# The first norm and the projections of a time-mixing layer as one stage by blocks of 512 tokens, with the attention's bias lines made in the low-rank stage

## The reference

```
h   = x * rsqrt(mean(x*x, channels) + 1e-6) * norm_w
dx  = shift(h) - h                  # h of the token before, zero ahead of token 0
r, k, v = (h + dx*mu_i) @ w_in[i]   # 1024 x 1024 each
g   = silu((h + dx*mu_g) @ w_in[3])
decay, a = functions of low-rank products (rank 64) of h and dx
```

## Time and profile before

| what | value |
|---|---|
| three runs | 3332.02, 3344.9, 3361.51 us; median 3344.9 |
| the profiled execution's own time | 3351.66 us |
| its span, first to last instruction | 3349.6 us |
| mean granted TensorE clock | 0.931 of full speed |
| PE, DVE, ACT, POOL busy | 88%, 48%, 33%, 17% of the span |

### The profile page before, as it was taken

One profiled execution on the slowest core, in us unless ns is written; L12 is line 12 of the kernel. 1 busy time (PEld: TensorE's weight loads), 2 busy tenths in 40 slices (PEclk: granted clock), 3 DMA queues, 4 the chain that ended last, 5 costly groups with the idle time before them and its releaser, 6 DMA issues. The chain is left out here.

```text
span 3349.6 us, 79029 instructions
## 1 busy us (share of the span) xinstructions
PE 2946.6 (88%) x35086; PEld 2442.5 (73%) x35086; DVE 1591.4 (48%) x2641; ACT 1098.3 (33%) x2020; POOL 564.3 (17%) x379
## 2 busy tenths in 40 slices
PE   4599999998858888888876997999799997999699
PEld 1487888887547778778775775888677887777587
DVE  4423232342256666666763662222277402767672
ACT  2223332221644443544533441111032212545410
POOL 0222222210012322223220220000000000034231
PEclk8799999999969888898997998999899998999899
DMA  5213341211462323323213761101111215223672
GB/s 161 79 51 99 106 125 61 79 60 58 135 183 80 97 66 91 91 74 97 67 53 102 222 193 32 38 32 37 38 57 57 82 64 190 84 73 97 219 239 85
DMA packets 339816, 322.65 MB, mean 96 GB/s; under 512 B 13935, under 2 KB 257007, under 8 KB 337824
## 3 DMA queue, kind: packets, MB, share of 16 engines
q1 hardware_dynamic: 312528, 263.55, 25.6%
q10 hardware_dynamic: 23904, 46.16, 3.9%
q0 software_dynamic: 3056, 8.05, 1.0%
HBM read 199.77 MB, written 122.64 MB: 96 GB/s over the span
## 5 line engine op out<-in xcount | busy, mean ns | idle before, releaser
L343 PE MATMUL pj_ps<-pj_x_hi,pj_w_hi 128*128 128x512 f32 x1024 | 402.2, 393 | 69.9 <-DVE pj_x_lo L298 61.4
L343 PE MATMUL pj_ps<-pj_x_lo,pj_w_hi 128*128 128x512 f32 x1024 | 400.9, 392 | 0.0
L343 PE MATMUL pj_ps<-pj_x_hi,pj_w_lo 128*128 128x512 f32 x1024 | 400.8, 391 | 0.0
L343 PEld LDWEIGHTS pj_ps<-pj_x_hi,pj_w_hi 128*128 128x128 f32 x1024 | 193.8, 189 | 114.5 <-DVE pj_x_lo L298 62.6
L277 POOL TENSOR_TENSOR pj_x<-h 128x512 f32<-128x512 f32 x128 | 168.0, 1313 | 578.1 <-DVE pj_x_lo L298 515.6
L298 DVE TENSOR_TENSOR pj_x_lo<-pj_x,pj_x_hi 128x512 fp32r<-128x512 f32 x128 | 89.1, 696 | 356.6 <-ACT pj_x_hi L353 356.6
L343 PEld LDWEIGHTS pj_ps<-pj_x_lo,pj_w_hi 128*128 128x128 f32 x1024 | 193.9, 189 | 40.3
L343 PEld LDWEIGHTS pj_ps<-pj_x_hi,pj_w_lo 128*128 128x128 f32 x1024 | 193.6, 189 | 40.4
L2190 DVE CUSTOM_DVE_ANT_0 wa_sc<-wa_sps,wa_table 128x256 f32<-128x256 f32 (+2 forms) x384 | 124.0, 360 | 144.4 <-PE wa_sps L2121 144.3
L1666 PE MATMUL cv_ps<-h_hi,cv_w_hi 128*128 128x512 f32 x512 | 158.6, 391 | 20.8 <-DVE cv_w_lo L1709 20.8
L804 ACT CAST rw_x<-rw_ps 128x512 f16<-128x512 f32 x160 | 96.2, 601 | 201.8 <-PE rw_ps L1110 201.7
(11 more groups left out here) (260 smaller groups left out, 6468.0 us busy)
## 6 DMA issues: line engine op xcount, KB each, us to landing
proj<-pj_out ACTq DMA_DIRECT2D x128, 256.0 KB, 2.5
pj_w<-w_in SPq DMA_DIRECT2D x32, 512.0 KB, 4.1
proj<-lr_out SPq DMA_DIRECT2D x32, 512.0 KB, 4.5
no_w<-w_out SPq DMA_DIRECT2D x32, 512.0 KB, 5.2
partial<-wa_ob SPq DMA_DIRECT2D x48, 264.0 KB, 2.1
mo_part<-partial SPq DMA_DIRECT2D x16, 792.0 KB, 9.2
wa_vt<-v_rows SPq DMA_DIRECT2D x43, 260.0 KB, 3.4
h<-xT SPq DMA_DIRECT2D x8, 1024.0 KB, 13.0
```

The source lines that it names most:

```text
L343: mm = pe.matmul(ps[i][:], wp, xp, start=k == 0 and m == 0, stop=k == KT - 1 and m == len(parts) - 1)
```

## The change

norm_phase and rwkv_projections become `normed_projections`. h is loaded by blocks: SP loads blocks 0 and 1 as eight tiles of 128 x 512 each with the first tile of weights between them; POOL issues blocks 2 and 3 as one DMA each, block 2 once block 0 has landed and block 3 once block 1 has. The squares of blocks 0 and 1 are ACT's, summed by 16 calls on PE as before; those of blocks 2 and 3 POOL makes and adds up itself in steps 0 to 15 of q = 0, so that PE has one call each. The root is exp(-0.5 ln(.)) on ACT in PSUM; DVE scales from PSUM. Blocks 2 and 3 are scaled at steps 8 and 16. One output buffer serves the first 17 steps, as the other holds squares. The bias lines and the skew table move into rwkv_low_rank: PE makes the lines between down 0 and down 1, DVE copies them between its parts of h for blocks 0 and 1, POOL issues the DMAs. `basic` is loaded in the recurrence's start, and the block that zeroed column 0 is gone.

The diff, without the deleted norm_phase (shown above) and with the waits on `s_const` in the recurrence cut (48 becomes 64 in each engine):

```diff
-def rwkv_projections(nc, h, vec, w_in, proj):
+def normed_projections(nc, src, h, gain, vec, w_in, proj):
         w_hi = sb("w_hi", [128, KT, KT, 128], F32R)
...
         scaled = sb("scaled", [128, QT])
+        sq = [scaled, out_sb[1]]
+        ones, eps = sb("ones", [128, 128]), sb("eps", [128, 1])
         ps = [c.enter_context(nc.psum_tensor(f"pj_ps{i}", [128, QT], F32)) for i in range(2)]
+        var = [c.enter_context(nc.psum_tensor(f"pj_var{i}", [128, QT], F32)) for i in range(4)]
+        s_first = [[sem(f"h{b}{k}") for k in range(KT)] for b in range(2)]
+        s_last = [sem(f"h{b}") for b in range(2, 4)]
+        s_zero, s_ones, s_square, s_summed, s_part, s_total, s_log, s_rstd, s_normed = (sem(n) for n in (
+            "zero", "ones", "square", "summed", "part", "total", "log", "rstd", "normed"))
         s_diff, s_x, s_x_hi, s_x_lo, s_w_hi, s_w_lo = (sem(n) for n in ("diff", "x", "x_hi", "x_lo", "w_hi", "w_lo"))
...
+        def out_of(n):
+            return n % 2 if n > 2 * KT else 0
+        def tokens(b):
+            return slice(1 + QT * b, 1 + QT * (b + 1))
         def next_input(q, r, last):
...
             def difference(k, quarter, n):
                 t0 = quarter * QT
-                pool.wait_ge(s_x_lo, n)
+                if n < 4 * KT:
+                    pool.wait_ge(s_normed, n + 1)
+                pool.wait_ge(s_x_lo, n + 1)
                 pool.tensor_tensor(x[k % 2][:], h[:, k, t0:t0 + QT], h[:, k, t0 + 1:t0 + QT + 1],
...
             def body(q, r, last):
                 if at := next_input(q, r, last):
-                    difference(at[0], at[1], at[2] + 1)
+                    difference(at[0], at[1], at[2])
+                if q == 0 and r < 2 * KT:
+                    squares(2 + r // KT, r % KT)
+            def squares(b, k):
+                at = (2 * KT - 1) * (b - 2) + 2 * k
+                part = h[:, k, tokens(b)]
+                if k == 0:
+                    pool.wait_ge(s_last[b - 2], 16)
+                    if b == 2:
+                        pool.wait_ge(s_summed, 2 * KT)
+                    else:
+                        pool.wait_ge(s_total, 1)
+                    pool.tensor_tensor(sq[1][:], part, part, ALU.mult).then_inc(s_part, 1)
+                else:
+                    pool.wait_ge(s_part, at - 1)
+                    pool.tensor_tensor(sq[0][:], part, part, ALU.mult).then_inc(s_part, 1)
+                    pool.wait_ge(s_part, at)
+                    pool.tensor_tensor(sq[1][:], sq[1][:], sq[0][:], ALU.add).then_inc(s_part, 1)
+            pool.memset(ones[:], 1.0).then_inc(s_ones, 1)
+            pool.memset(eps[:], EPS).then_inc(s_ones, 1)
+            pool.memset(h[:, :, 0:1], 0.0).then_inc(s_zero, 1)
+            pool.wait_ge(s_zero, 1)
+            for b in range(2, 4):
+                pool.wait_ge(s_first[b - 2][KT - 1], 16)
+                pool.dma_start(h[:, :, tokens(b)], src[:, :, QT * b:QT * (b + 1)]).then_inc(s_last[b - 2], 16)
             pool.sem_inc(s_x_lo, 2)
             for k in range(KT):
-                difference(k, 0, k + 1)
+                difference(k, 0, k)
             blocks(pool, body)
         @block.vector
         def _(dve):
-            def mix(k, quarter, n, column):
-                i, t0 = quarter % 2, quarter * QT
+            def scale(b, k):
+                part = h[:, k, tokens(b)]
+                dve.wait_ge(s_rstd, b + 1)
+                dve.scalar_tensor_tensor(part, part, gain[:, k:k + 1], var[b][:],
+                                         ALU.mult, ALU.mult).then_inc(s_normed, 1)
+            def blend(k, quarter, n, column):
+                t0 = quarter * QT
                 dve.wait_ge(s_diff, n + 1)
...
                                          h[:, k, t0 + 1:t0 + QT + 1], ALU.mult, ALU.add).then_inc(s_x, 1)
+            def rest(k, quarter, n, column):
+                i = quarter % 2
                 dve.wait_ge(s_x_hi, n + 1)
...
             def body(q, r, last):
+                if q == 0 and r in (KT, 2 * KT):
+                    for k in range(KT):
+                        scale(1 + r // KT, k)
                 if at := next_input(q, r, last):
-                    mix(*at)
+                    blend(*at)
+                    rest(*at)
                 if at := next_weights(q, r, last):
...
+            def first(k):
+                return k, 0, k, V["mu_r"] + k
+            scale(0, 0)
+            scale(0, 1)
             weights(0, 0)
             for k in range(KT):
-                mix(k, 0, k, V["mu_r"] + k)
-            for j in range(1, FIRST):
+                blend(*first(k))
+                if k + 2 < KT:
+                    scale(0, k + 2)
+                rest(*first(k))
+            weights(0, 1)
+            weights(0, 2)
+            for k in range(KT):
+                scale(1, k)
+            for j in range(3, FIRST):
                 weights(0, j)
...
         def _(sp):
...
             sp.sem_inc(s_w_lo, 1)
-            with sp.Fori(0, 4) as q:
+            for b in range(2):
+                for k in range(KT):
+                    sp.dma_start(h[:, k, tokens(b)], src[:, k, QT * b:QT * (b + 1)]).then_inc(s_first[b][k], 16)
+                if b == 0:
+                    sp.dma_start(w[:], w_cols[:, :, 0:128]).then_inc(s_w, 16)
+            for j in range(1, KT):
+                sp.wait_ge(s_w_lo, j + 1)
+                sp.dma_start(w[:], w_cols[:, :, j * 128:j * 128 + 128]).then_inc(s_w, 16)
+            with sp.Fori(1, 4) as q:
                 for j in range(KT):
...
                 mm.then_inc(s_mm, 1)
+                if q == 0 and r in (KT - 1, 2 * KT - 1):
+                    b = 2 + r // KT
+                    pe.wait_ge(s_part, (2 * KT - 1) * (b - 1))
+                    pe.matmul(var[b][:], ones[:], sq[1][:], start=True, stop=True).then_inc(s_total, 1)
+            pe.wait_ge(s_ones, 2)
+            for b in range(2):
+                for k in range(KT):
+                    n = b * KT + k
+                    pe.wait_ge(s_square, n + 1)
+                    pe.matmul(var[b][:], ones[:], sq[n % 2][:], start=k == 0, stop=k == KT - 1).then_inc(s_summed, 1)
             blocks(pe, body)
         @block.scalar
...
+            def squares(b):
+                for k in range(KT):
+                    n = b * KT + k
+                    act.wait_ge(s_first[b][k], 16)
+                    if n >= 2:
+                        act.wait_ge(s_summed, n - 1)
+                    act.activation(sq[n % 2][:], h[:, k, tokens(b)], ACT.Square).then_inc(s_square, 1)
+            def inverse_root(b):
+                if b < 2:
+                    act.wait_ge(s_summed, KT * (b + 1))
+                else:
+                    act.wait_ge(s_total, b - 1)
+                act.activation(var[b][:], var[b][:], ACT.Ln, scale=1.0 / D, bias=eps[:]).then_inc(s_log, 1)
+                act.wait_ge(s_log, b + 1)
+                act.activation(var[b][:], var[b][:], ACT.Exp, scale=-0.5).then_inc(s_rstd, 1)
             def weights(q, j):
...
             def body(q, r, last):
+                if q == 0 and r in (KT, 2 * KT):
+                    inverse_root(1 + r // KT)
                 if at := next_input(q, r, last):
...
                 i, n = r % 2, q * PER + r
+                o = out_of(n)
                 act.wait_ge(s_mm, n + 2)
-                act.wait_ge(s_out[i], q * (8 * PER) + (16 * (r // 2) + 16))
+                act.wait_ge(s_out[o], 16 * sum(out_of(m) == o for m in range(n)) + 16)
+                if n == 2 * KT + 1:
+                    act.wait_ge(s_total, 2)
                 if last:
-                    act.activation(out_sb[i][:], ps[i][:], ACT.Sigmoid).then_inc(s_sig, 1)
+                    act.activation(out_sb[o][:], ps[i][:], ACT.Sigmoid).then_inc(s_sig, 1)
                 elif q == 1:
                     act.wait_ge(s_scaled, 16 * r)
-                    act.copy(out_sb[i][:], ps[i][:])
+                    act.copy(out_sb[o][:], ps[i][:])
                     act.activation(scaled[:], ps[i][:], ACT.Copy,
...
                 else:
-                    act.copy(out_sb[i][:], ps[i][:]).then_inc(s_ps_free, 1)
+                    act.copy(out_sb[o][:], ps[i][:]).then_inc(s_ps_free, 1)
                 act.wait_ge(s_ps_free, n + 3)
                 t0, j = r // KT * QT, r % KT
-                act.dma_start(proj_rows[q, :, j, t0:t0 + QT], out_sb[i][:]).then_inc(s_out[i], 16)
+                act.dma_start(proj_rows[q, :, j, t0:t0 + QT], out_sb[o][:]).then_inc(s_out[o], 16)
                 if q == 1:
...
             act.sem_inc(s_out[1], 16)
+            act.preload_act_table_set("natural_log_exp_and_others")
+            act.wait_ge(s_ones, 2)
+            squares(0)
+            inverse_root(0)
             weights(0, 0)
+            squares(1)
+            inverse_root(1)
             for k in range(KT):
...
             for i in range(2):
-                act.wait_ge(s_out[i], 8 * 4 * PER + 16)
```

(62 more changed lines are left out.)

84 lines of the change are left out of this document (removed).

## The result

| kernel | median of its runs | ratio to before, 95% interval |
|---|---|---|
| before, 4 runs | 3339.11 us (3332.02 to 3361.51) | 1 |
| changed, 4 runs | 3307.11 us (3291.77 to 3310.65) | 0.9879 [0.9836, 0.9922] |
| changed, once more, 5 runs | 3296.76 us | 0.9875 [0.9853, 0.9898] |

The ratio says 1.2% faster, some 40 us, with an interval clear of 1. The medians of the first set lie 32 us apart; in the second set the kernel before had 3341.44, so 45 us.

A forecast was written before the change was run, and what follows sets the result against it. PE bounds the kernel, so an earlier first product moves everything behind it: -62.5 + 1.9 + 2 + 3.3 + 3 + 0.5 = -51.8 us, 3299.9 for the profiled execution, median 3293, range 3275 to 3322.

The forecast's parts named there:

- The term for the table: Low-rank stage: skew table's DMAs meet the stores, part absorbed by ACT running four stores ahead; +3 us, bounds 0 and 16.
- T0: Start of the projections' first product: 113.1 us before, forecast 50.6 once it hangs on block 1, 62.5 us earlier.
- first steps: First 16 projection steps: two ones calls +1.9 us; ACT's first copy 0 to 3 us later, taken as +2.
- the 40 to 65: Whole kernel: the forecast's own band for the gain in us, given a chance of 0.71.
- Steps 8 and 16: Projections: root and eight scalings delay ACT's copy but cost PE nothing, with 1.9 us to spare.
- Lines: Low-rank stage: PE makes bias lines after down 0, then waits for DVE's copy and first part of block 1; +3.3 us.
- `basic`: Recurrence's start: loading it there costs one issue and a wait, +0.5 us (0 to 1).
- Its signs: Trace marks expected, among them a PE gap of about 3 us after down 0 and longer store waits in raised 0 only.
- 1: Rival: slow front (T0 57), steps losing 8 us and stores 16, all together; gain 21.8, time 3323; chance 0.17.
- the half-way case: Half of the way to the slow front and starved stores: time 3308 us.
- 2: Rival: block 1 lands late, crowded out by POOL's transfers; T0 68 or later, gain some 35 us, 3310; chance 0.05.
- 3: Rival: POOL bounds steps 0 to 15 through the port shared with DVE; slower, 3427 at steps of 13.8 us; chance 0.04.

The follow-up runs named there:

- `early_lines`: Changed kernel, but PE makes the bias lines before down 0 and ACT, not DVE, copies them out; ratio to before 0.9845, 3290.74 us.
- `pool_more`: Changed kernel with five more unread POOL multiplications of 128x192 in 14 of steps 0 to 15; ratio to before 0.9939, 3321.25 us.
- `weights_early`: `first_high` with weights 1 and 2 also split among the first mixes; ratio to before 0.9839, 3290.05 us.
- `first_high`: Changed kernel, but ACT alternates first high parts with block 1's squares and POOL issues block 3 after eight differences; ratio to before 0.9863, 3296.31 us.
- `best`: `weights_early` with `early_lines`, the skew table issued by SP ahead of its first store; ratio to before 0.9812, 3277.88 us.

## Why the prediction was right

The time was given as 3293, range 3275 to 3322, for a gain of 51.8; the first set of runs has its median at 3307, with a lowest run of 3292. Direction and range held, and so did the mechanism of the start. The term for the table did not, and luck hid part of that: T0 and the first steps came out 5.7 us better than forecast and paid for half of the 10.9 us that the table cost more. A gain of 32 by the medians or 40 by the ratio lies below or at the lower edge of the 40 to 65 that the forecast gave 0.71. Step by step:

- **T0**, forecast 50.6, measured 46.8. Block 0's sums took 7.19 to 17.5 (forecast 7.2 to 18.4), block 1's 16 records 9.1 us, 0.57 each in place of 0.70: the slow rate of the earlier trace rows belongs to the first records only. In block 0 the calls (two records each) began 1.7 to 1.8 us apart at first and 0.95 at the end; in block 1, where the granted clock was 0.50 at first (20 to 22), only the first two took 1.9 and 1.3. Block 1 had landed by 23.6 (forecast 25 to 28), so its loads bound nothing. The mixing took 16.1 us, and the 0.5 us for DVE's added scalings did not show. A gain of 66.3 instead of 62.5 in this pair; T0 was 44.4 to 48.6 over the profiles with this start.
- **First steps**, forecast +2 for the copy: 0, since PE waited 3.99 us for it, as it had 4.1. The ones calls were given +1.9; the whole stage from first to last product start is 2.0 longer.
- **Steps 8 and 16**, forecast nothing with 1.9 us to spare: PE did not wait. POOL's step was forecast at 3.1 to 4.4 us and is 4.8: nearer to 5.44 than I had it, and still free.
- **Lines**, +3.3: measured 3.6, and gone when they were moved ahead (`early_lines`). In four other profiles with the lines in this place, the second of the changed kernel among them, low 1 came 16.3 us behind low 0 instead of 14.8, so 5.1: there the granted clock fell behind PE's pause at the lines (0.77 in 790 to 795 of that second profile, where the first has 1.00 in 795 to 800).
- **The table, +3, is the term that was mis-sized**: the low-rank stage lost 17.5 us, 3.6 of them by the lines, 13.9 by the table, near the upper bound of 16. "ACT may run four stores ahead ... so part is absorbed" failed. Four buffers are eight passes of 0.59 us, 4.7 us of work; the prediction had read the sum of the queue's time well, and not asked how long the *first* stores would take in such company: 22.7 us. The overlap was, if anything, put too long: the table began 5.4 us behind low 0 instead of 9.4, since the lines landed 2.6 us after their issue and not 5.9, and so it had 11.8 us ahead of the first store instead of 8. Its choice of 3 leaned on a count of buffers, when the row nearest to the case was the table's own share.
- By the Trainium skill ("DMA: Bandwidth & Descriptors", section "SWDGE vs HWDGE vs iDMA") the queues take turns, and the prediction read half speed for the stores out of it. The trace does not bear out the half: the stores moved 0.82 of 2.87 MB in those 16 us, 29%, and 0.05 MB a us where it had been 0.29. Early in the same profile it does come out: in 14 to 24, when POOL's queue loads block 2 and SP's block 1, they moved 1.99 and 1.90 MB. So equal turns are not refuted in general; the table beside the stores didn't get them, and why is open.
- **`basic`**, +0.5: the stretch that holds it came out 1.2 shorter, and varies by 16 us between profiles, so its size can't be read.
- **Its signs**: a PE gap behind down 0 (792.98 to 796.41, 2.1 us of it the lines) was there, and the waits for stores were longer than before in raised 0 only, as it said.

Forecast terms and measured ones: -62.5 against -66.3, +3.9 against +2.0, +3.3 against +3.6, +3 against +13.9; the sum is -51.8 against about -47, and the attention's clock took another 7 from this pair.

Rivals: 1 had the right place for its 16 us, but needed the slow front as well, which was not there; the half-way case that it named, 3308, is where the time came out, for other reasons. 2 fell with T0. 3 has its edge, if that is PE's step, 0.6 us away; the point from which it would have eaten the gain lies 3.2 us above PE's step, and `pool_more`, beyond the edge, was still faster than before.

## What to carry to other kernels

A bulk transfer that nobody waits for is free only as long as no small, urgent one shares the engines with it: ask of every place you might put it which load or store comes next there and how many buffers stand between that and the bound engine. Here the same 4.7 MB cost 14 us beside stores, 16 beside the first weights of a stage, and nothing that showed once one wait put it behind them. And when the start of a chain is pulled forward, the next thing in line (here the copy behind three weight tiles through a single buffer and block 1's scalings) decides how much of it arrives: `weights_early` finished 7 us earlier than `first_high` with a later T0.

## What the runs showed of the hardware

- The same DRAM to DRAM copy took 12.4 KB a us of each engine from POOL's queue and 19.9 from ACT's (0.14 and 0.17 MB a us in all), but its three issues held POOL for 3.20 us and ACT for 13.04 (SP, in `best`: 13.17).
- Beside the table on POOL's queue a store of 512 KB landed after 22.7 us instead of 5.0.
- PE's clock fell to the lower level, 0.50, in 820 to 825, when PE had stood without work since 815.0.
- Window attention's first 20 us ran at 0.50 in one profile of the changed kernel and at 0.91 in the other, and its first part took 115.9 and 108.0 us.
